# The last down-projection block and its norm by token halves between two decoder layers

## What is computed

```
for i in range(2):
    h = x @ w_in            # many column groups; the first are q_idx, k_idx, ka, va, w_idx (452 columns)
    ...                     # attention, convolution, merge
    x = layer_norm(ALPHA * x + merged @ w_out, ln1_g, ln1_b)
    f_gate, f_up = split(x @ w_ffn_in)
    ffn = (silu(f_gate) * f_up) @ w_ffn_out          # 2816 -> 1024, the down-projection
    ple = sigmoid(x @ w_ple_gate) * (p_i @ w_ple_proj)
    x = layer_norm(ALPHA * x + ffn + ple, ln2_g, ln2_b)
```

## Time and profile before

| | |
|---|---|
| median of 3 runs | 1756.22 us (1755.61 to 1756.75) |
| the profiled execution | 1755.99 us |
| its span, first to last instruction | 1753.9 us |
| mean granted clock of TensorE | 0.997 |
| busy, share of the span | PE 99%, DVE 72%, ACT 58%, POOL 59% |

### The profile page before, as it was taken

The page is one execution under the profiler, slowest core; times in us unless marked ns, Lnnn a source line. Parts: engine busy times, 40 slices in busy tenths (PEclk is TensorE's granted clock), DMA queues, the critical chain, the costliest instruction groups (busy, mean ns, idle before and its releaser), DMA issues. The chain is left out here.

```text
span 1753.9 us, 27631 instructions
## 1 busy us (share of the span) xinstructions
PE 1732.4 (99%) x9074; PEld 1475.8 (84%) x9074; DVE 1264.0 (72%) x2517; ACT 1011.6 (58%) x1963; POOL 1037.5 (59%) x686
## 2 busy tenths in 40 slices
PE   9999999999999999999999999999999999999997
PEld 8878888888888888888898788888887898888887
DVE  7279889877799888813363888897878998887034
ACT  4555887843476776722244558877445676766223
POOL 5446679654436777754434466895543367777542
PEclk9999999999999999999999999999999999999998
DMA  5323221223232323243323343122332332322332
GB/s 180 99 90 126 84 76 61 71 86 96 97 120 97 121 97 117 77 128 100 97 80 103 97 119 91 59 70 65 99 102 96 101 117 98 120 97 97 120 102 67
DMA packets 51558, 171.82 MB, mean 98 GB/s; under 512 B 6368, under 2 KB 8672, under 8 KB 51424
## 3 DMA queue, kind: packets, MB, share of 16 engines
q1 hardware_dynamic: 50560, 168.84, 29.6%
q10 hardware_dynamic: 864, 1.28, 0.3%
HBM read 162.76 MB, written 2.10 MB: 94 GB/s over the span
## 5 line engine op out<-in xcount | busy, mean ns | idle before, releaser
L699 POOL TENSOR_TENSOR sb_wl<-sb_wraw,sb_wh 128x1024 fp32r<-128x1024 f32 x205 | 498.1, 2434 | 486.9 <-ACT sb_wh L862 475.3
L862 ACT ACTIVATE sb_wh<-sb_wraw 128x1024 fp32r<-128x1024 f32 x199 | 210.3, 1058 | 262.5 <-PE banks L1316 151.6
L1314 PE MATMUL banks<-sb_x_both,sb_wh 128*128 128x512 f32 (+1 forms) x672 | 267.9, 399 | 5.9 <-DVE sb_u L2447 3.6
L1316 PE MATMUL banks<-sb_x_both,sb_wl 128*128 128x512 f32 (+1 forms) x672 | 253.3, 377 | 0.0
L1315 PE MATMUL banks<-sb_x_both,sb_wh 128*128 128x512 f32 (+1 forms) x672 | 252.6, 376 | 0.0
L1757 PE MATMUL banks<-sb_t_both,sb_wh 128*128 128x512 f32 x640 | 174.7, 394 | 0.0
L2039 DVE TENSOR_TENSOR sb_u<-sb_u,banks 128x512 f32<-128x512 f32 x31 | 21.3, 687 | 186.6 <-PE banks L1316 186.6
L1314 PEld LDWEIGHTS banks<-sb_x_both,sb_wh 128*128 128x128 f32 x672 | 127.0, 189 | 27.5 <-issue 7.9
L1316 PEld LDWEIGHTS banks<-sb_x_both,sb_wl 128*128 128x128 f32 x672 | 126.5, 188 | 24.2
L1936 DVE SCALAR_TENSOR_TENSOR banks<-sb_hconv,sb_par,banks 128x512 f32<-128x512 f32 x192 | 142.7, 743 | 0.5
L1314 PE MATMUL banks<-sb_hh,sb_wh 128*128 128x512 f32 (+1 forms) x374 | 142.3, 380 | 0.1
(11 more groups left out here) (397 smaller groups left out, 4620.7 us busy)
## 6 DMA issues: line engine op xcount, KB each, us to landing
sb_wraw<-in_weights SPq DMA_DIRECT2D x256, 512.0 KB, 3.5
sb_wraw2a<-in_weights SPq DMA_DIRECT2D x24, 512.0 KB, 3.5
sb_wraw2b<-in_weights SPq DMA_DIRECT2D x24, 512.0 KB, 4.4
sb_u<-in_x SPq DMA_DIRECT2D x8, 256.0 KB, 7.2
sb_q_raw<-sb_qn_t SPq DMA_DIRECT2D x16, 128.0 KB, 2.2
sb_k_raw<-sb_kn_t SPq DMA_DIRECT2D x16, 128.0 KB, 2.3
out<-sb_u SPq DMA_DIRECT2D x16, 128.0 KB, 1.9
sb_q_raw<-sb_qr_t SPq DMA_DIRECT2D x16, 64.0 KB, 2.0
```

The lines of the kernel that those rows point to most:

```text
L699: nc.gpsimd.tensor_tensor(wl[:, t % WS, :], wraw[:, t % 2, :], wh[:, t % WS, :].bitcast(F32), ALU.subtract).then_inc(lo_ready, 1)
L862: nc.scalar.activation(wh[:, t % WS, :], wraw[:, t % 2, :], ACT.Copy).then_inc(hi_ready, 1)
L1314: nc.tensor.matmul(out, wh_, xh_, start=start, stop=False, skip_group_check=onto)
L1316: return nc.tensor.matmul(out, wl_, xh_, start=False, stop=stop, skip_group_check=onto)
```

## The change

The last down-projection block and the norm of layer 0 take the way of layer 1's tail, by token halves, and the first token projection of layer 1 runs for one half after the other. TensorE's `tail` serves both layers; in layer 0 the second half's statistics are issued inside the next layer's `first_group`, after its k = 0, 2 and 5 (first half). The fills of this norm go away. VectorE and ScalarE get a `next_input` each, in which the second half's statistics stand between the first half's blocks. Counters (U_READY, Z_READY and so on) count the added steps; three PSUM banks of the tail have other numbers, in layer 1 too. ScalarE makes the high of tile 0 in the k loop and those of tiles 1 to 6 inside `next_input`.

```diff
-TAIL_MEAN, TAIL_SCALE, TAIL_SQUARE, TAIL_PRODUCT = (6, 5), (7, 1), (2, 0), (3, 4)
+TAIL_MEAN, TAIL_SCALE, TAIL_SQUARE, TAIL_PRODUCT = (6, 7), (5, 4), (2, 3), (3, 4)
 TAIL_STEPS = {5: "mean", 8: "squares", 12: "scale"}
+HEAD_STEPS = {0: "mean", 2: "squares", 5: "scale"}
...
ScalarE
+            def half_square(layer, h):
+                ...
+                nc.scalar.activation(sq[1][:, 0, cols], u[:, DK - 1, cols], ACT.Square).then_inc(squared, 1)
...
+            def half_high(layer, h, j):
+                cols = token_half(h)
+                act.wait_ge(z_ready, layer * Z_READY + (DK + DK * h + j + 1))
+                nc.scalar.activation(xh[:, j, cols], u[:, j, cols], ACT.Identity,
+                                     bias=column("l2b", j)).then_inc(x_high, 1)
+
+            def next_input(layer, first):
+
+                half_square(layer, 0)
+                half_deviation(layer, 0)
+                high(1, first + TILES)
+                half_high(layer, 0, 0)
+                high(2, first + TILES)
+                for j in range(1, DK):
+                    half_high(layer, 0, j)
+                    if j == 2:
+                        half_square(layer, 1)
+                        high(3, first + TILES)
+                    elif j == 5:
+                        half_deviation(layer, 1)
+                for j in range(DK):
+                    half_high(layer, 1, j)
+                    if j in (3, 5, 7):
+                        high(4 + (j - 3) // 2, first + TILES)
...
-                        if layer == 0 or n > 0:
+                        if layer == 0 or n > 3:
                             high(n + LEAD, first)
...
-                    elif T_FO + k + LEAD < TILES or layer < L - 1:
+                    elif T_FO + k + LEAD < TILES + (layer < L - 1):
                         high(T_FO + k + LEAD, first)
...
-                    squares(layer, 1, DK - 1)
-                    deviation(layer, 1)
-                    high(LEAD, first + TILES)
-                    for j in range(DK):
-                        norm_high(layer, 1, j)
+                    next_input(layer, first)
...
TensorE
+            def first_group(layer, first):
+
+                name, ncol, nk, _ = TOKEN_GROUPS[0]
+                for half in range(2):
+                    for k in range(DK):
+                        t, kk = k // nk, k % nk
+                        if half == 0 and kk == 0:
+                            arrived(t, first)
+                        pe.wait_ge(x_ready, (layer - 1) * Z_READY + (2 * DK + DK * half + k + 1))
+                        ...
+                        for b in range(2 * half, 2 * half + 2):
+                            o, rows = psum[:, b, 0:ncol], slice(b * P, b * P + P)
+                            nc.tensor.matmul(o, xh[:, k, rows], h, start=(k == 0), stop=False)
+                            nc.tensor.matmul(o, xh[:, k, rows], lw, start=False, stop=False)
+                            last = nc.tensor.matmul(o, xl[:, k, rows], h, start=False, stop=(k == DK - 1))
+                        if half == 1 and kk == nk - 1:
+                            last.then_inc(tile_used, 1)
+                        if half == 0 and k in HEAD_STEPS:
+                            tail_stats(layer - 1, 1, HEAD_STEPS[k])
...
-                for what in TAIL_STEPS.values():
-                    tail_stats(layer, 1, what)
+                if layer == L - 1:
+                    for what in TAIL_STEPS.values():
+                        tail_stats(layer, 1, what)
...
-                    if layer == L - 1 and j == DK - 1:
+                    if j == DK - 1:
                         tail(layer, first)
                         break
...
-                if layer < L - 1:
-                    norm(layer, 1)
...
VectorE
+            def next_input(layer, whole, total, squares):
+
+                base = layer * Z_READY + 2 * DK
+
+                def low(h, j):
+                    cols = token_half(h)
+                    dve.wait_ge(x_high, base + (DK * h + j + 1))
+                    v.scalar_tensor_tensor(xl[:, j, cols], u[:, j, cols], column("l2b", j), xh[:, j, cols].bitcast(F32),
+                                           ALU.add, ALU.subtract).then_inc(x_ready, 1)
+
+                half_sums(layer, whole, 0, total)
+                half_squares(layer, 0, squares)
+                half_means(layer, 0)
+                half_variance(layer, 0)
+                half_diagonal(layer, 0, squares)
+                for h in range(2):
+                    dve.wait_ge(mean_spread, layer * NORMS + (h + 2))
+                    centered = [half_center(h, j) for j in range(EARLY)]
+                    dve.wait_ge(spread, layer * NORMS + (h + 2))
+                    for j in range(DK):
+                        steps.reached(centered[j])
+                        half_scale(h, j)
+                        if j + EARLY < DK:
+                            centered.append(half_center(h, j + EARLY))
+                        if j > 0:
+                            low(h, j - 1)
+                        if h == 0 and j == 1:
+                            half_sums(layer, whole, 1, total)
+                        elif h == 0 and j == 2:
+                            half_squares(layer, 1, squares)
+                        elif h == 0 and j == 3:
+                            half_means(layer, 1)
+                        elif h == 0 and j == 4:
+                            half_variance(layer, 1)
+                        elif h == 0 and j == 6:
+                            half_diagonal(layer, 1, squares)
+                    low(h, DK - 1)
```

More of the change, by code:

```diff
@@ L1341, in group @@
                 name, ncol, nk, tiles = TOKEN_GROUPS[g]
+                if layer > 0 and g == 0:
+                    if part == 0:
+                        first_group(layer, first)
+                    return
                 if part == 0:
@@ L1974, in attention, with half_sums @@
                 steps.end("V_ATTN", V_ATTN)
-            def tail(layer, whole, h, total, squares):
-                cols, blocks, n = token_half(h), slice(2 * h, 2 * h + 2), layer * 2 + (h + 2)
+            def half_sums(layer, whole, h, total):
+                cols = token_half(h)
                 product = psum[:, TAIL_PRODUCT[h], cols]
[L1980 to L1984, removed]
                 if h == 0:
-                    dve.wait_ge(half_used, 1)
+                    dve.wait_ge(half_used, layer + 1)
                 else:
@@ L2011, in tail @@
+            def tail(layer, whole, h, total, squares):
+                half_sums(layer, whole, h, total)
+                half_squares(layer, h, squares)
+                half_means(layer, h)
+                half_variance(layer, h)
+                half_diagonal(layer, h, squares)
+                dve.wait_ge(mean_spread, layer * NORMS + (h + 2))
                 dve.wait_ge(mean_copied, h + 1)
-                for j in range(EARLY):
-                    center(j)
+                centered = [half_center(h, j) for j in range(EARLY)]
@@ L2014, in tail @@
                 steps.wait()
-                dve.wait_ge(spread, n)
+                dve.wait_ge(spread, layer * NORMS + (h + 2))
                 for j in range(MINE):
@@ L2019, in tail @@
                     if j >= EARLY:
-                        steps.wait(back=min(EARLY - 1, MINE - 1 - j))
-                    v.scalar_tensor_tensor(u[:, j, cols], u[:, j, cols], column("l2g", j), scale, ALU.mult,
-                                           ALU.mult).then_inc(z_ready, 1)
+                        steps.reached(centered[j])
+                    half_scale(h, j)
                     if j + EARLY < MINE:
-                        center(j + EARLY)
+                        centered.append(half_center(h, j + EARLY))
             def norm(layer, n, start, tile):
-                x0, g, b = layer * 16 + 8 * n, ("l1g", "l2g")[n], ("l1b", "l2b")[n]
-                last = n == 1 and layer == L - 1
+                u0 = layer * U_READY + 8 * n
+                halves = n == 1
                 total, squares = sums[n][:, 0], sums[n][:, 1]
@@ L2070, in norm @@
                 dve.wait_ge(shifted, layer * 8 + (4 * n + 4))
-                for j in range(2, DK - 1 if last else DK):
+                for j in range(2, DK - 1 if halves else DK):
                     if j >= 4:
@@ L2085, in norm @@
                         add_square(k)
-                if last:
+                if halves:
+                    whole = first + (tile(DK - 1) + 1 + START)
+                    if layer < L - 1:
+                        next_input(layer, whole, total, squares)
+                        return
                     for h in range(2):
-                        tail(layer, first + (tile(DK - 1) + 1 + START), h, total, squares)
+                        tail(layer, whole, h, total, squares)
                     return
@@ L2476, in _ @@
                 norm(layer, 1, lambda j: None, lambda j: T_FO + PARTS * j + PARTS - 1)
[L2477 removed]
```

(1 more changed line is left out.)

131 lines of the change are left out of this document (77 added, 54 removed).

## The result

The changed kernel takes 1761.03 us (median of 8 runs, 1759.31 to 1763.31) beside 1755.91 of the kernel before on the same chip (8 runs, 1754.69 to 1757.59): ratio 1.003, with an interval of 1.002 to 1.0039. It is slower by some 5 us, where 1757.1 was forecast, "no change" had 0.77, and the range ended at 1758.5. The profiled execution took 1759.31, with a span of 1757.5.

A forecast was written before the change was run, and what follows sets the result against it. TensorE was taken to bound the kernel, busy 1732.4 of 1753.9 us. Boundary work of 39.19 instead of 43.62 saves 4.43, waits add 5.35: +0.9 on 1756.22 gives 1757.1 us, range 1752.5 to 1758.5.

The forecast's parts named there:

- no change: Whole kernel: measured time not told apart from the kernel before, bounds 1752.7 and 1759.7 us; chance 0.77.
- TensorE's own work, 39.19 us: Layer boundary without waits: down-projection by halves 17.56, token projection 19.91, second half's statistics 1.72.
- The ceiling of 4.43: Layer boundary: the most the change can save without a wait, 43.62 - 39.19 us, 0.25% of the time.
- The waits of the first half: Token projection, first half: TensorE waits for low parts at k = 1, 2 and 3, of 0.40, 0.35 and 1.40 us.
- the sum: Layer boundary: waits of 5.35 us against 4.43 saved, so +0.9 us.
- 1.75 and 1.45: Token projection, second half: TensorE's waits at k = 4 and 5, as GpSimd's weight lows hold VectorE's low parts.
- VectorE behind GpSimd: Low parts: a VectorE instruction with two SBUF operands waits until a running GpSimd subtraction (2.40 us) is over.
- (1): Low parts: the hold is not on the path, only 0.75 of waits stay, 1752.5 us; chance 0.11.
- (2): First half's statistics: only the two-column mean product is not held, 0.8 less, 1756.3 us; chance 0.20.
- the third wait: First half, k = 3: 1.40 us, from the two-column product held behind GpSimd's low of tile 3; bounds 0 and 1.40.
- Rival (3), the clock: Second half's gaps, about 889.8 to 894.3: TensorE's clock falls, three steps at half speed add 3.7, 1760.8 us; chance 0.10.
- Behind the boundary: Layer 1's tail: costed at nothing, since only bank numbers and counters change there.

The follow-up runs named there:

- The last version: Mended kernel plus highs of tiles 4 to 6 after all activation highs, mean product with a bank operand, GpSimd's low of tile 3 in four pieces: 1752.13 us, 0.9973.
- the kernel with three waits: Mended kernel plus ScalarE's highs of tiles 4, 5 and 6 after all eight activation highs of the second half: 1752.89 us, ratio 0.9977.
- the mended kernel: Changed kernel with highs of tiles 1 and 2 waiting only for the tile four before, not every tile of the layer: 1756.23 us, ratio 0.9998.
- the product free: Mended kernel plus VectorE's two-column mean times mean reading one factor from the PSUM bank: 1754.93 us, ratio 0.9992.
- the kernel with the four pieces: Mended kernel plus GpSimd's lows of tiles 4 and 5 in four pieces of 256 columns each: 1752.83 us, ratio 0.9977.
- the 15 fills: Changed kernel plus 15 useless small TensorE matmuls between the last down-projection matmul and the token projection's first wait: 1760.37 us, ratio 1.0025.

## Why the prediction was wrong, point by point

- **TensorE's own work, 39.19 us: right.** The last version's boundary of 40.19 has two waits, which count 0.54 and 0.45 from start to start (each 0.16 more than the idle time in the row): 40.19 - 0.99 = 39.20. From the kernel with three waits, 41.40 - 2.08 = 39.32; the next point has what these counts leave out, some 0.1 a wait. The ceiling of 4.43 was real.
- **The waits of the first half: the step that failed** is "Tile 1's high, which the old k loop did during the product, now waits behind the first half's deviation: 866.06". I took the place in the queue for the whole condition, and did not work out the semaphore value of the call with its new arguments. In the changed kernel it starts at 870.71. That one wait costs 44.37 to 48.68, 4.31 us, partly as the gap before the projection, partly because GpSimd's lows of tiles 1 and 2 then fall onto low parts 0 and 1 (2.27 and 1.21).
- With that call as I had read it, the mended kernel, **the sum holds**: its boundary is 44.37 where 39.19 + 5.35 = 44.5 was forecast. The waits count, from start to start, 0.54, 0.45 and 1.09 for 0.40, 0.35 and 1.40, and 1.58 and 1.17 for 1.75 and 1.45. They sum to 4.83, and 44.37 - 39.19 - 4.83 = 0.35 is left. TensorE's rows hold about that much behind the waits: the matmul after a waited one follows 0.28 to 0.32 later instead of 0.21 (at the last wait 893.53, 893.85, 894.05). The mended kernel's time cannot be told from that of the kernel before, 0.9998, where "the same" had been forecast.
- **VectorE behind GpSimd: right**, at 256 columns (2.31, 2.20) and at two (2.14). The rule of the Trainium skill's page "SBUF — State Buffer" (section "SBUF: two separate sides"), an exclusive lock for two SBUF inputs and for the whole instruction, names no least size, and these rows agree. So rivals (1) and (2) fall. One bound was wrong in the forecast itself: for the third wait it names 0 as the lower one, while its own working takes 0.8 from 1.40 and so leaves 0.6. With the product free, the trace shows no wait there.
- **Rival (3), the clock**: it did fall, and the forecast had it in the wrong half. In the profile of the change it fell in the first half, where it costs 0.2 to 0.3; in one of the experiments in the second half, for 1.4. Its 1760.8 comes near the result by another cause. The forecast's sign of this rival, a granted clock below 1 before 897 and a time over 1759, was thus met without being its proof. That the clock's cost comes and goes is shown by a pair of rows. Every kernel here, the one before included, has a wait of 1.75 to 1.80 near 1400. In one execution the clock is down behind it, in another not:

```profile
1395.02 0.36 PE L1360 MATMUL banks<-sb_x_both,sb_wh 128*128 128x256 f32 x1 [1.75 <-DVE sb_u L2588]
1395.00:1398.40 3.40, 3.38 (x17) 3.40 (x18) 3.40 (x7) 1.27 (x3) 1.35 (x2) 0.54 0.09 16
```

```profile
1398.51 0.36 PE L1346 MATMUL banks<-sb_x_both,sb_wh 128*128 128x256 f32 x1 [1.76 <-DVE sb_u L2574]
1398.50:1401.90 3.40, 3.39 (x28) 3.40 (x29) 3.40 (x7) 1.71 (x4) 1.35 (x2) 1.00 0.13 22
```

The first pair is from the kernel with the four pieces, the second from the mended one. The mean granted clock of every run is on record too. In the ten runs of the unedited change it goes from 0.992 to 0.995, and a run is longer by 1.5 us for each 0.001 that it lies lower, by 1.2 to 1.4 in the kernel before: much of the spread between runs of one kernel goes with the clock. It is not the main reason why the change is slower: the 15 fills raised the mean from 0.994 to 0.996 and took only 1.0 us off the median, while the mended wait took off 5.1 at nearly the same mean, 0.9965.
- **Behind the boundary** I had forecast no difference. The change's group starts 4.64 later than before and the span ends only 3.6 later. Set matmul by matmul against the kernel before, TensorE is 0.42 ahead at the start of the block (run by run: the first loads), 0.2 is regained at a wait near 1061, and 0.7 at one place, where the kernel before had this wait:

```profile
1381.26 0.36 PE L1314 MATMUL banks<-sb_x_both,sb_wh 128*128 128x256 f32 x1 [0.53 <-DVE sb_th L2349]
```

It is absent from the profiles of the change and of all experiments but the last version, which waits 1.0 there. The wait hangs on ScalarE, which stood 2.04 us for the DMA of `sb_wraw2b` before and 0.86 after. Why that load is earlier was not traced; it stays open. From the group to layer 1's tail the mended kernel takes 825.23 us and the kernel before 826.23; this 1.0, most of it at this place, balances a boundary that is 0.75 longer, in these two profiles. Both differences are smaller than what the runs can tell. Between the medians, the clamped wait costs 5.1 us (1761.37 to 1756.23, each about its own kernel before the same to 0.02), between the boundaries 4.31; the rest is within the spread of the runs.

## What to carry to other kernels

When a call moves to another place, work out the value that its semaphore wait then has: a helper's clamp or base count can turn "four tiles back" into "everything before", and a stalled copy takes along whatever is queued behind it. Give VectorE's serial steps either a GpSimd that has nothing large to run then, or short GpSimd instructions, or one operand in a PSUM bank. And before a lower clock is blamed, see in the same window which engine is busy without a pause.

## What the runs showed of the hardware that was not expected

The size of VectorE's instruction does not matter to the hold: one of two columns took 2.14 us instead of 0.16. It is the length of GpSimd's instruction, and what of it is left when VectorE comes, that matters: with 256 columns (0.8 us each) in place of 1024 (2.4), the hold fell from 2.31 to 0.67. And 6.8 us at half the clock, amid the busiest stretch of the boundary, cost 0.2 to 0.3 us, since VectorE was the one that others waited for. A wait of 1.75 us was followed by a granted clock of 0.54 in one execution, and one of 1.76 at the same place by 1.00 in another.
